# Dealing the last expert unit's pieces anew among the steps of the second block

## What is computed

```python
act = gelu(einsum('td,ted->te', tb, expert_u[eb]))        # a dot product of a token with each of its 128 u rows
out = einsum('te,ted->td', gb * act, expert_v[eb])        # the weighted sum of the 128 v rows
```

```python
z = rms_norm(h, attn_norm_g[l]) @ w_in[l]                 # c_q, c_kv, k_pe, rq, rk, rv, rg
y = concat([mla_mixer(...), retention_mixer(...)]) @ w_out[l]
h = h + y
gate, up = split(rms_norm(h, ffn_norm_g[l]) @ w_gate_up[l])
h = h + (silu(gate) * up) @ w_down[l]
```

## Time and profile before

| | |
|---|---|
| time, median of 3 runs | 2556.39 us (2556.32 to 2560.9) |
| profiled execution, its time | 2560.87 us |
| its span | 2559.1 us |
| TensorE busy | 2221.8 us, 87% |
| VectorE busy | 1559.0 us, 61% |
| ScalarE busy | 452.5 us, 18% |
| GpSimd busy | 627.7 us, 25% |
| moved by DMA | 900.98 MB, mean 352 GB/s |

### The profile page before, as it was taken

One profiled execution on the slowest core, in us unless ns is written; L12 is line 12 of the kernel. 1 busy time (PEld: TensorE's weight loads), 2 busy tenths in 40 slices (PEclk: granted clock), 3 DMA queues, 4 the chain that ended last, 5 costly groups with the idle time before them and its releaser, 6 DMA issues.

```text
span 2559.1 us, 40369 instructions
## 1 busy us (share of the span) xinstructions
PE 2221.8 (87%) x16556; PEld 2054.0 (80%) x16556; DVE 1559.0 (61%) x4112; ACT 452.5 (18%) x985; POOL 627.7 (25%) x518
## 2 busy tenths in 40 slices
PE   9998889878879978788987898877988889999999
PEld 6897779877768978767987876877857888899799
DVE  1248577686776967857778697684877633211310
ACT  1211133011123111013301222100221011201200
POOL 0013323343333334332334222232222200000000
PEclk9999889989989989898998887998979899999999
DMA  8489999999999999999999987999978968468474
GB/s 305 166 345 421 421 363 392 422 420 421 421 417 384 422 420 421 421 421 368 379 422 420 396 350 264 377 422 392 385 278 322 424 241 361 167 242 309 146 262 153
DMA packets 105590, 900.98 MB, mean 352 GB/s; under 512 B 12572, under 2 KB 15680, under 8 KB 16704
## 3 DMA queue, kind: packets, MB, share of 16 engines
q0 software_dynamic: 73904, 537.43, 51.6%
q1 hardware_dynamic: 30400, 357.95, 35.6%
q10 hardware_dynamic: 1104, 3.02, 0.3%
HBM read 897.30 MB, written 1.05 MB: 351 GB/s over the span
## 4 chain that ended last, share of the span: by engine, by line
PE 44%; DMA 28%; DVE 22%; issue 4%; ACT 1%; POOL 1%; SPq 0%; DVEq 0%; ACTq 0%
DMA row<-in_experts,idx 15%; PE ea L916 11%; PE pa L916 10%; DMA wring<-in_weights 7%; DMA more<-in_experts,idx 7%; DVE row L1924 6%; PE ea L836 4%; PE pa L756 4%; PE pa L665 4%; DVE acc L1907 3%; PE s L692 1%; DVE topi L1816 1%; DVE more L1924 1%; PE pa L924 1%; DVE idxf L1871 1%
## 5 line engine op out<-in xcount | busy, mean ns | idle before, releaser
L2323 POOL DMA_INDIRECT row<-in_experts,idx x448 | 548.5, 1224 | 1279.7 <-DVE acc L1907 609.0
L1924 DVE CUSTOM_DVE_ANT_0 row<-row,h2n 128x1024 f32<-128x1024 f32 x448 | 533.6, 1221 | 156.7 <-DMA row<-in_experts,idx 155.6
L836 PE MATMUL ea<-diag,row 128*128 128x128 f32 x3808 | 499.9, 296 | 146.5 <-DVE diag L1946 146.5
L836 PEld LDWEIGHTS ea<-diag,row 128*128 128x128 f32 x3808 | 488.5, 212 | 159.6 <-DVE diag L1946 159.6
L1907 DVE SCALAR_TENSOR_TENSOR acc<-row,wgt,acc 128x1024 f32<-128x1024 f32 x207 | 265.3, 1281 | 1.7
L1421 ACT ACTIVATE gl<-dots 128x4 f32<-128x4 f32 x128 | 26.3, 206 | 965.8 <-DVE dots L1924 965.7
L916 PE MATMUL ea<-hB,wring 128*128 128x144 f32 (+1 forms) x1120 | 160.2, 309 | 33.7 <-DMA wring<-in_weights 29.9
L916 PEld LDWEIGHTS ea<-hB,wring 128*128 128x128 f32 x1120 | 156.2, 212 | 37.9 <-DMA wring<-in_weights 31.9
L756 PEld LDWEIGHTS pa<-hA,wring 128*128 128x128 f32 x960 | 122.1, 206 | 15.6 <-issue 12.6
L756 PE MATMUL pa<-hA,wring 128*128 128x128 f32 x960 | 134.2, 297 | 0.0
L916 PE MATMUL pa<-hB,wring 128*128 128x144 f32 (+1 forms) x992 | 127.3, 290 | 4.5 <-DMA wring<-in_weights 4.5
(11 more groups left out here) (539 smaller groups left out, 3180.7 us busy)
## 6 DMA issues: line engine op xcount, KB each, us to landing
wring<-in_weights SPq DMA_DIRECT2D x111, 2048.0 KB, 11.5
wlate<-in_weights SPq DMA_DIRECT2D x25, 2048.0 KB, 8.1
wring<-in_weights SPq DMA_DIRECT2D x22, 1408.0 KB, 7.2
wlate<-in_weights SPq DMA_DIRECT2D x10, 1408.0 KB, 6.4
more<-in_weights SPq DMA_DIRECT2D x5, 2048.0 KB, 7.9
row<-in_experts,idx POOLq DMA_INDIRECT x448, 17.4
row<-in_weights SPq DMA_DIRECT2D x3, 2048.0 KB, 18.1
wring<-in_weights SPq DMA_DIRECT2D x3, 1792.0 KB, 10.3
```

Source lines behind the costliest of these rows:

```text
L836: m = pe.matmul(EA[c // 4][:, (c % 4) * P:(c % 4 + 1) * P], v[:, c * P:(c + 1) * P], diag[:, DIAG_SLOTS * (q % 2) + i, :], start=False, st ...
L1924: dve.tensor_tensor_reduce(out=r, in0=r, in1=h2n[:, u % 2, :], scale=1.0, scalar=0.0, op0=ALU.mult, op1=ALU.add, accum_out=dots[:, g % 2, ...
L2323: pool.indirect_dma_start(out=expert_rows[slot], out_offset=None, in_=table, in_offset=bass.IndirectOffsetOnAxis(ap=idx[:, k % 2, GB * g + ...
```

## The change

The shares become two lists, one for unit 0 and one for unit 1, and two `yield`s of VectorE's `layer2` move: `gate_scaled(0)` goes from the end of step 11 to the start of step 12, `gate_scaled(1)` from the end of step 13 to the start of step 14.

```diff
-SHARE2 = ([0.6, 1.8, 0.8, 0.8, 0.9, 0.8, 1.8, 1.8, 1.6, 1.2, 1.6, 1.6, 1.0, 1.8, 1.0, 1.0, 1.0, 1.0, 1.0, 1.6, 1.6, 0.9, 0.6]
-          + [1.4] + [2.1] * (FC // 2 - 1) + [1.4] * KC)
-STEPS2 = len(SHARE2)
+SHARE2 = {0: ([2.2, 1.8, 0.8, 0.8, 0.9, 0.8, 1.8, 1.8, 1.6, 1.2, 1.6, 1.6, 3.6, 1.8, 1.0, 1.0, 2.6, 1.0, 1.0, 2.4, 2.2, 4.0, 0.0]
+              + [0.9] + [1.35] * (FC // 2 - 1) + [0.9] * KC),
+          1: ([0.6, 1.8, 0.8, 0.8, 0.9, 0.8, 1.8, 1.8, 1.6, 1.2, 1.6, 1.6, 2.2, 1.8, 3.4, 1.0, 2.6, 1.0, 1.0, 1.6, 2.4, 4.9, 0.0]
+              + [0.9] + [1.35] * (FC // 2 - 1) + [0.9] * KC)}
+STEPS2 = len(SHARE2[0])
...
-    share = SHARE2 + SHARE2[:STEPS2 - KC]
+    share = SHARE2[0] + SHARE2[1][:STEPS2 - KC]
...
                 probs(1)
                 if not t:
                     centered("rvm", rvm[l][:], META, 2)
+                yield
                 gate_scaled(0)
-                yield
                 logits(3)
...
                 probs(3)
                 decayed(1)
+                yield
                 gate_scaled(1)
-                yield
                 decayed(2)
```

## The result

The changed kernel takes 2565.6 us (median of 7 runs, 2558.55 to 2570.84) beside 2556.4 for the kernel before: the ratio is 1.0031, with an interval of 1.0017 to 1.0045. It is slower by 0.3%, where 2531.4 and "faster" were forecast. The profiled execution took 2565.6 us, its span 2563.8, 4.7 more than before.

A forecast was written before the change was run, and what follows sets the result against it. The prediction took VectorE to bound attention until about step 12 and DMA to bound feed-forward. Attention +12.8 and +3.5, feed-forward -28.5 and -12.8 summed to -25.0, from 2556.4 to 2531.4 us, range 2516 to 2549.

The forecast's parts named there:

- Gate/up: Unit 0's ten gate/up steps: fewer gathers make tiles land sooner, 90 us in place of 106.
- the same term: Unit 1's gate/up: 17 pieces fewer bring 98.8 us to 86, -12.8 us, ends -8 and -16.
- Rival 3: Feed-forward tiles' landing time does not fall, so it gains nothing and attention's +16.3 remain: 2573 us, chance 0.06.
- Step 0: Start of unit 0's attention: the fifth piece puts a gelu ahead of ScalarE's squares, root later by 7.3 us.
- Step 12: Unit 0's attention: eight pieces instead of two, 9.6 us instead of 2.3, third head's probabilities 11.4 us later.
- It has slack before the next product is needed: Unit 0's attention, steps 1 to 10: rvm may start near 1546 instead of 1535.68, behind the moved `best_experts`.
- rival 4: TensorE's slow clock spreads over attention from step 12 to 21, 14 us a unit: 2559 us, chance 0.05.
- Unit 1's attention: Unit 1's attention stage: 22 us of extra work mostly fits the waits, +3.5 us, ends -2 and +9.
- a freed row has 15 us until its dot product: Rows freed before step 20 have 15 us against a landing of 16.0; taken as 0, up to +4.
- rival 2: VectorE's lumps cost their full length in attention, +19 and +9, with the middle of the gains: 2543 us, chance 0.13.
- signs of being wrong: In the profile after: a gate/up step over 10 us, new row waits in attention, unit 0's first root at 1464.
- slower as soon as the feed-forward gives back less than 16.3: Whole kernel: the change turns slower if feed-forward gives back less than 16.3 of its forecast 41.3 us.

The follow-up runs named there:

- run 4: Changed kernel with unit 0 dealt as in the kernel before and seven pieces before unit 1's step 21 instead of eleven: 2548.7 us, ratio 0.9956 to the kernel before.
- run 5: The two moved yields alone, with the old deal of the kernel before: 2555.0 us, ratio 0.9991.
- run 6: Changed kernel with unit 0 as before but four pieces fewer in its last down steps, unit 1 exactly as changed: ratio 1.0012 to the kernel before.
- run 7: As run 6, but seven pieces before unit 1's step 21 instead of eleven and four more beside its gate/up: ratio 0.9995 to the kernel before.
- run 11: Unit 0's old deal with seven gate/up pieces taken out, more before steps 14, 16, 21, none before 22; unit 1 as run 4: 2540.2 us, ratio 0.9926.
- run 12: Both units from the old deal, with three pieces before step 14, five before 16, seven before 21, none before 22: 2538.1 us, ratio 0.9913.
- run 8: Changed kernel with one piece before unit 0's step 0 and two before step 12, ten pieces going to gate/up and down: ratio 0.9956 to the kernel before.
- run 1: Changed kernel with one piece before unit 0's step 0 instead of five, four going to its last down steps: ratio 0.9992 to the kernel before.
- run 2: Changed kernel, same deal, but ScalarE does unit 0's step 0 behind one piece and its other four afterwards: ratio 1.0 to the kernel before.
- run 3: Unit 0 as in the changed kernel, unit 1 as in the kernel before with four pieces more beside gate/up: ratio 1.0034 to the kernel before.
- run 10: Changed kernel with 15 pieces beside unit 0's gate/up instead of 30, the other 15 moved before step 21: 2584.23 us in total.
- run 9: Changed kernel with no piece beside unit 0's gate/up, all 30 moved before step 21: 2597.95 us in total.

## Why the prediction was wrong

**Gate/up, the larger part of the error.** The step that failed is "With a landing of 9.5 to 10 us a gate/up step is 8.8 to 9.1". The rule in it, that a step is the mean of landing and matmul time, is right: after, (11.1 + 8.7) / 2 = 9.9 against 10.0 measured, with 8.7 as TensorE's busy time of a step, and before, (12.3 + 8.7) / 2 = 10.5 against 10.6; in the other kernels whose landings are on record it comes within 0.5 us of the step. The landing was mis-sized, 9.5 to 10 for 11.1, and the matmul time a little, 8.1 for 8.7. I had taken the stretch as bound by bytes and let each of 8.5 rows give back its 2.5 us. But only 4.8 rows' worth of bytes left the ten steps, and a row gives back 2.5 us only while the DMA engines are full. Afterwards they are not (384 GB/s), and still six of the ten steps wait for their tile. All the kernels together:

| pieces beside unit 0's gate/up | ten steps, us | 2 MB tile lands, us | gathers, MB | GB/s |
|---|---|---|---|---|
| 47 (before, runs 4 to 7) | 105.8 to 110.9 | 12.1 to 12.3 | 24.0 to 26.1 | 415 to 422 |
| 40 (runs 11, 12) | 100.8, 100.3 | 11.8, not recorded | 20.8, 20.5 | 410 |
| 36 (run 8) | 105.6 | not recorded | 21.8 | 404 |
| 30 (changed, runs 1, 2, 3) | 99.9, 99.9, 101.3, 104.0 | 11.1, 11.2, 11.5, 11.8 | 19.0, 18.2, 17.6, 17.6 | 384, 390, 378, 368 |
| 15 (run 10) | 86.3 | not recorded | 9.2 | 323 |
| 0 (run 9) | 82.5 | 7.9 | 2.4 | 254 |

From 47 pieces to 30 the ten steps lose 6 to 8 us, where 16 were forecast, and the median landing of a 2 MB tile is never under 11.1. Only far below, at 15 and 0 pieces, do they come near TensorE's 81. Between 40 and 30 pieces no gain can be told. For unit 1 the same term was 86 us and measured 96.4 (the forecast had also cut that stage at 2063, 5.8 us before its end, which are 104.6 us before the change). Rival 3, in which landings don't fall at all, was the near miss: they fell by half of what was assumed, and run 9 shows that the gathers are indeed what lengthens them.

**Step 0.** Mechanism and place were right: a gelu ahead of the squares, +7.3 us. The squares are 11.5 us later, the root 11.3: 1.0 is a later start of the unit in this profile, 3.0 are three waits for rows (0.55 + 1.16 + 1.25), since four dot products now come earlier than their rows. The forecast had set 0 for late rows, "up to +4".

**Step 12, the rest of unit 0's attention.** The forecast for the whole stage was +12.8, 5.5 of it behind the root; in the profiles it is +22.8, 11.6 behind the root. What failed is the path up to the third head. The forecast had those probabilities 11.4 us late: 7.3 for the root, 7.3 for the lump, less some that small waits would swallow. They are 20.6 late:

```profile
1555.13 0.69 PE L979 MATMUL ptb<-kst,soft 128*128 128x128 f32 x2 [0.21 <-DVE soft L2057]
```

```profile
1551.74 0.69 PE L981 MATMUL ptb<-kst,soft 128*128 128x128 f32 x2 [7.15 <-DVE soft L2059]
...
1553.62 9.37 PE L926 MATMUL pa<-wring,hB 128*16 128x512 f32 x16
...
1575.73 0.69 PE L981 MATMUL ptb<-kst,soft 128*128 128x128 f32 x2 [5.61 <-DVE soft L2059]
```

The first row is of the kernel before, the others of the changed one. The root's 11.3 and the lump's 7.3, paid in full (experiment 8), make 18.6 of them: nothing was swallowed, and 2 were added. The sentence "It has slack before the next product is needed" was wrong. `best_experts` ahead of head 0's probabilities leaves TensorE idle for 7.15 us, the product rvm starts at 1553.62 and not near 1546, and VectorE waits 4.0 us for it (the wait at L2029 above), right ahead of the lump. In experiment 1, where `best_experts` stands behind those probabilities, neither wait is there.

Part of that wait is TensorE's clock. The product rvm took 9.37 us in the changed kernel and 7.04 before. The granted clock was 0.75 of full speed in the 9.37 us, 0.50 in the 1.9 us ahead of them, and 1.00 in the 7.04 us before the change, so TensorE was at the lower of its levels, 1.2 GHz, for a part of them, behind an idle stretch of 7.15 us. The Trainium skill, "TensorE: Matmul & The Clock Gate", section "HAM oscillation — how this bites in real kernels", says that TensorE falls back to half rate in the gap before the next group of matmuls, there a wait for DMA, and that this group starts slow. The trace agrees, with 2.3 us at this place, where the gap is a wait for VectorE. The forecast named the clock as rival 4 at its extreme and put nothing for it into the sum.

**Unit 1's attention.** Forecast +3.5, end +9, measured +7.7. The step-by-step sum was right where rows were there: run 4, with seven pieces at step 21, has the stage at +0.4. What failed is the sentence that a freed row has 15 us until its dot product: three waits for rows, 6.0 us, and TensorE behind them. The forecast looked at the lump before step 21 alone and took 0; there the wait is 2.0 us, and 4.0 stand in the pieces before step 16, which it didn't look at.

**What was right**: that VectorE's work fits into its waits at steps 14, 16 and 21 (runs 11, 12), that the lumps before steps 0 and 12 are on the path (runs 1, 2, 8), and the sign of each stage. Two of the forecast's own signs of being wrong came, a gate/up step that still takes 10 us and waits for rows in attention. Attention came out near rival 2 (+19 and +9), the feed-forward's gain between that rival's low ends (20 and 8 us) and rival 3's nothing. The error of the total is the sum of two errors of one sign: 17 us too much gain in feed-forward (24.2 instead of 41.3) and 14.2 too little price in attention (30.5 instead of 16.3). The decision point "slower as soon as the feed-forward gives back less than 16.3" was reckoned with attention's price fixed; both moved.

## What to carry to other kernels

Fill a wait only with what it holds, and look at what the added work brings on the other engines that share the order: here one piece too many ahead of a step brought another engine a wait ahead of the critical chain. When work is taken out of a bandwidth-bound stretch, count the bytes that really leave it, not the pieces (pieces done just before it send their gathers into it), and count them only down to the point where the queues stop being full; behind it the time is set by how long one transfer takes, and perhaps by the number of places for it, which no run here varied. With a ring of prefetched rows, shift the pieces by half a group and look at the rows again, since two deals with the same counts can differ by 8 us. And before a deal is changed, write out where the few long pieces (`best_keys`, `best_experts`) come to stand.

## What the runs showed of the hardware

The landing of a 2 MB weight tile goes from 7.9 us with hardly a gather beside it to 12.3 us beside 26 gathers of 1 MB, and it is still 11.1 us beside 16, when the engines move 384 GB/s and are busy 0.94 of the time. Why it stays that long when the engines are no longer full is open: which gathers meet which tile was not tried, and four kernels with the same 30 pieces in the ten steps range from 99.9 to 104.0 us.
